# Three projections of a fused two-block layer in staggered runs: the second 128 tokens four weight pieces behind the first

## The reference, cut to what matters

```python
merged = sigmoid(ga) * (ya @ w_branch_a) + sigmoid(gb) * (yb @ w_branch_b)
mix_out = merged @ w_out
ple = sigmoid(x @ w_ple_gate) * (p @ w_ple)
x = layer_norm(DEEPNORM_ALPHA * x + mix_out + ple, ln_g, ln_b)      # end of block 1
...
h = rms_norm_2(x, g_mix_norm) * (1.0 + scale_m) + shift_m           # block 2
proj = h @ w_in                 # columns 0..415 and 1952..1959 are the narrow block "c0"
```

## Time and profile before

| | us |
|---|---|
| median of 3 runs | 1148.98 (1148.11 to 1151.58) |
| profiled execution, its own time | 1146.6 |
| its span | 1144.9 |
| PE busy | 1062.0 (93% of the span) |
| DVE busy | 550.1 (48%) |
| ACT busy | 390.1 (34%) |
| POOL busy | 335.6 (29%) |
| DMA | 320.65 MB, 280 GB/s over the span |

### The profile page before, as it was taken

The page is one execution under the profiler, slowest core; times in us unless marked ns, Lnnn a source line. Parts: engine busy times, 40 slices in busy tenths (PEclk is TensorE's granted clock), DMA queues, the critical chain, the costliest instruction groups (busy, mean ns, idle before and its releaser), DMA issues. The chain is left out here.

```text
span 1144.9 us, 12825 instructions
## 1 busy us (share of the span) xinstructions
PE 1062.0 (93%) x4990; PEld 705.6 (62%) x4990; DVE 550.1 (48%) x987; ACT 390.1 (34%) x668; POOL 335.6 (29%) x261
## 2 busy tenths in 40 slices
PE   6999999989999696999987999999999999999993
PEld 4887888768877565887776635353544444444442
DVE  5978677758765766655644312222222122222214
ACT  4645675546433424657333211121111111111212
POOL 1058946594683057274400000000000000000000
PEclk9999999989998797999996999999999999999997
DMA  9656653956675264455349389999999999999991
GB/s 327 207 184 221 221 202 111 338 178 252 199 275 186 74 194 147 128 172 204 112 185 376 120 343 416 412 417 418 417 418 417 417 416 417 416 417 417 418 374 38
DMA packets 93933, 320.65 MB, mean 280 GB/s; under 512 B 6288, under 2 KB 7328, under 8 KB 76976
## 3 DMA queue, kind: packets, MB, share of 16 engines
q1 hardware_dynamic: 92832, 316.07, 72.3%
q0 software_dynamic: 752, 3.22, 0.8%
q10 hardware_dynamic: 288, 0.52, 0.1%
HBM read 318.74 MB, written 1.05 MB: 279 GB/s over the span
## 5 line engine op out<-in xcount | busy, mean ns | idle before, releaser
L757 PE MATMUL ps<-hl,L 128*128 128x512 f32 (+1 forms) x1216 | 389.0, 402 | 11.8 <-DVE rlo L1501 8.5
L757 PEld LDWEIGHTS ps<-hl,L 128*128 128x128 f32 x1216 | 232.5, 194 | 60.9 <-issue 14.6
L1501 DVE TENSOR_TENSOR rlo<-ring,hl 128x1024 fp32r<-128x1024 f32 (+1 forms) x154 | 209.0, 1376 | 119.5 <-ACT hl L1164 118.7
L757 PE MATMUL ps<-rlo,L 128*128 128x512 f32 (+1 forms) x608 | 241.1, 397 | 0.0
L757 PE MATMUL ps<-slots_all,xe 128*64 128x512 f32 (+1 forms) x1056 | 226.9, 582 | 0.8 <-DVE rt L2236 0.8
L1164 ACT ACTIVATE hl<-ring 128x1024 fp32r<-128x1024 f32 (+1 forms) x154 | 159.9, 1057 | 196.6 <-PE ps L757 79.3
L718 POOL TENSOR_SCALAR ring<-ring,st 128x512 f32<-128x512 f32 x84 | 168.8, 2009 | 0.0
L746 POOL CAST two<-ident 64x128 fp32r<-64x128 f32 x64 | 19.1, 298 | 501.1 <-PE ps L757 499.6
L757 PEld LDWEIGHTS ps<-slots_all,xe 128*64 128x64 f32 x1056 | 73.9, 137 | 131.7 <-issue 128.5
L757 PEld LDWEIGHTS ps<-rlo,L 128*128 128x128 f32 x608 | 117.3, 193 | 25.0
L720 POOL TENSOR_TENSOR macc<-macc,ring 128x512 f32<-128x512 f32 x84 | 119.4, 1421 | 7.0
(11 more groups left out here) (208 smaller groups left out, 902.2 us busy)
## 6 DMA issues: line engine op xcount, KB each, us to landing
slots_all<-in_w_exp_gate SPq DMA_DIRECT2D x64, 1024.0 KB, 20.0
slots_all<-in_w_exp_up SPq DMA_DIRECT2D x64, 1024.0 KB, 15.9
slots_all<-in_w_exp_down SPq DMA_DIRECT2D x64, 1024.0 KB, 16.7
ring<-in_w_in SPq DMA_DIRECT2D x49, 1024.0 KB, 5.4
ring<-in_w_mod SPq DMA_DIRECT2D x24, 1024.0 KB, 7.3
ring<-in_w_out SPq DMA_DIRECT2D x8, 1024.0 KB, 5.1
ring<-in_w_ple_gate SPq DMA_DIRECT2D x4, 1024.0 KB, 5.2
ring<-in_w_branch_a SPq DMA_DIRECT2D x4, 1024.0 KB, 6.1
```

Of the source, the lines that this page charges most:

```text
L757: return e.matmul(o, l, r, start=start, stop=stop)
L1501: return e.tensor_tensor(o, a, b, op)
```

## The change

Names form runs: bb0 with bb1, wo0 with wo1, and c0 alone (`BEHIND`, lag 4). A run is a list of steps. In step s PE does piece s for m=0 and then piece s-4 for m=1. So a run of eight pieces has twelve steps: four with m=0 alone, four with both, four with m=1 alone; `c0` has eight steps. `pe_at`, `begun` and `used` give for every half its count and step; what frees a buffer is counted by `used`, the step in which m=1 has passed. The transposes, sums and norms are split by m and put between steps (`at`). The mean is a sum that DVE's addition accumulates, the variance a sum of squares by ACT with the mean as bias, and the last scaling isn't a DVE pass: `DIAG(m)`, the identity times 1/rms, is the moving operand of an ordinary float32 matmul that turns and scales R.

```diff
+        BEHIND = (("bb0 bb1", 4), ("wo0 wo1", 4), ("c0", 4),)
...
+                for s in range(len(ps) + lag):
+                    t = sum(len(v) for v in steps_of.values())
+                    halves = [(ps[s], 0)] if s < len(ps) else []
+                    halves += [(ps[s - lag], 1)] if s >= lag else []
+                    for g, m in halves:
+                        pe_at[(g, m)] = len(pe_at) + 1
+                        (used if m else begun)[g] = t
...
             if kind == "weights":
-                return last_piece[i] + 1
+                return used[last_piece[i]] + 1
...
-        for g in range(npieces):
+        for t, halves in (step for v in steps_of.values() for step in v):
             first = at_piece
-            while at_piece < min(g + NH, npieces) and all(
-                    freed_by(q) <= g for q in range(pieces[at_piece][0] - NS + 1)):
+            while at_piece < npieces and (at_piece < NH or used[at_piece - NH] < t) and all(
+                    freed_by(q) <= t for q in range(pieces[at_piece][0] - NS + 1)):
                 at_piece += 1
...
+            def spread_tokens(name, m, src, diag, ready):
+                for j0 in (0, 4):
+                    b = take((name, m, j0))
+                    ready(m, j0)
+                    for j in range(4):
+                        x = mm(b[:, 128 * j:128 * j + 128], src(m, j0 + j), diag(m), True, True)
+                    taken(x)
...
+            project("bb0", L0, l_ready("ybT"), {9: lambda: merged_turn(0)})
+            project("wo0", L1, l_ready("mT"), {1: lambda: merged_turn(1)})
+            h_turn(0)
+            project("c0", L0, h_ready, {2: lambda: h_turn(1)})
+            project("fq", L0, h_ready)
...
+            project("bb0", at={10: lambda: rounded("mT", tokens=(0,))})
+            def ln_square(m):
+                w.wait_ge(ln_v, 2 * m + 1)
+                act(UA[:, m, :], R[:, m, :], ACT.Square, bias=st[:, 74 + m:75 + m],
+                    accum_out=st[:, 168 + m:169 + m]).then_inc(ln_a, 1)
+                w.wait_ge(ln_v, 2 * m + 2)
                 act(st[:, 76 + m:77 + m], st[:, 76 + m:77 + m], ACT.Sqrt).then_inc(ln_a, 1)
...
+            project("wo0", at={2: first_rows, 7: lambda: ln_square(0), 8: first_squares, 9: roots})
+            h_round(0, 0)
+            square(1, 0)
+            h_round(0, 4)
+            square(1, 1)
+            square_root(1)
+            h_round(1, 0)
+            h_round(1, 4)
...
+            project("bb0", at={3: lambda: bb(0, 0), 7: after_bb1, 10: lambda: completed("mT", tokens=(0,))})
+            bb(1, 1)
...
+            def less_mean(m):
+                w.wait_ge(*evacuated("wo1", m))
+                mine(tt(st[:, 72 + m:73 + m], st[:, 160 + 2 * m:161 + 2 * m], st[:, 161 + 2 * m:162 + 2 * m], ALU.add))
...
+            def diagonal(m):
+                w.wait_ge(rt_a, m + 1)
+                mine(e.reciprocal(st[:, 70 + m:71 + m], st[:, 68 + m:69 + m]))
+                wait_mine()
+                tsc(DIAG(m), ident[:, :], st[:, 70 + m:71 + m], None, ALU.mult, None).then_inc(xn_set, 1)
...
+            def first_rows():
+                wo(1, 0)
+                less_mean(0)
+                variance(0)
+                wo(0, 1)
+                scale(0)
+                scaled(0, 0)
+                scaled(0, 1)
+
+            def second_rows():
+                w.wait_ge(sq_a, 2)
+                mean_square(0, rt_v)
+                wo(1, 1)
+                diagonal(0)
+                less_mean(1)
+                variance(1)
+                h_shift(0)
+                scale(1)
+                scaled(1, 0)
+                h_low(0, 0)
+                h_shift(4)
+                scaled(1, 1)
+                h_low(0, 4)
+
+            project("wo0", at={2: lambda: completed("mT", tokens=(1,)), 3: lambda: wo(0, 0), 7: first_rows, 9: second_rows})
+            w.wait_ge(sq_a, 4)
+            mean_square(1, rt_v)
+            diagonal(1)
+            h_low(1, 0)
+            h_low(1, 4)
```

More of the change, by code:

```diff
@@ L358, in two_blocks @@
         ev_a, ev_v = Events(sem("ev_a")), Events(sem("ev_v"))
-        for name in order:
-            for m in range(2):
+        for lead in steps_of:
+            for name, m in ((name, m) for m in range(2) for name in names_of[lead]):
                 dve = name.rstrip("01") in BY_DVE or (name in SHARED and m == 0)
@@ L413, in aux_turn, with aux_tokens, turn_order @@
                 aux((name, m, j0), by[n % len(by)])
+        def aux_tokens(name, m, by):
+            for j0 in (0, 4):
+                aux((name, m, j0), by)
+        BY_TOKENS = ("mT", "hT",)
+        def turn_order(name, groups):
+            if name in BY_TOKENS:
+                return [(j0, m) for m in range(2) for j0 in groups]
+            return [(j0, m) for j0 in groups for m in range(2)]
         HEADS_IN = {name: (s,) for s, name in enumerate("za1 ua0 ua1 va0 va1 zb0 zb1 gb0 gb1 ga0".split())}
@@ L499, in two_blocks @@
                              ("ofT", (0,)), ("mT2", (0, 4)), ("h3", (0, 4))):
-            for j0 in groups:
-                for m in range(2):
-                    th.add((name, m, j0))
+            for j0, m in turn_order(name, groups):
+                th.add((name, m, j0))
         for i in range(NP):
@@ L812, in between, with project @@
                     pair(4, FOX_IN[name][n], QM, KMT, 66, FV)
-            def project(name, L, ready):
-                for c in MOD_SUM.get(name, ()):
-                    mod_sum(c)
-                ps = blocks[name]
-                for n, g in enumerate(ps):
-                    w.wait_ge(hi, g + 1)
-                    w.wait_ge(lo, g + 1)
-                    hi_g, lo_g = hi_of(g), pieces[g][3]
-                    for m in range(2):
+            def project(lead, L, ready, at={}):
+                for name in names_of[lead]:
+                    for c in MOD_SUM.get(name, ()):
+                        mod_sum(c)
+                four = len(blocks[lead]) == 4
+                for s, (_, halves) in enumerate(steps_of[lead]):
+                    for g, m in halves:
+                        w.wait_ge(hi, g + 1)
+                        w.wait_ge(lo, g + 1)
+                        hi_g, lo_g = hi_of(g), pieces[g][3]
+                        name, n = block_of[g]
                         o = PS[bank_of[name] + m][:, 0:pieces[g][2]]
@@ L830, in project @@
                             mm(o, L[:, 1, kk, tok(m)], hi_g[:, k, :], False, False)
-                            x = mm(o, L[:, 0, kk, tok(m)], lo_g[:, k, :], False, kk == 2 * len(ps) - 1)
+                            x = mm(o, L[:, 0, kk, tok(m)], lo_g[:, k, :], False, kk == 2 * len(blocks[name]) - 1)
                         x.then_inc(pe_w, 1)
-                    if n == 1 and len(ps) == 4:
-                        between(name, 0)
-                between(name, 1 if len(ps) == 4 else 0)
+                    if s == 1 and four:
+                        between(lead, 0)
+                    if s in at:
+                        at[s]()
+                between(lead, 1 if four else 0)
             def scores(names, q, k, n):
@@ L1799, in head_norm, with completed @@
                     yield
-            def completed(name, groups=(0, 4)):
+            def completed(name, groups=(0, 4), tokens=(0, 1)):
                 for j0 in groups:
-                    for m in range(2):
+                    for m in tokens:
                         w.wait_ge(th.sem, th.at[(name, m, j0)])
@@ L1900, in _ @@
             project("ba1", branch("ba1", 1, GA, "ga1", None, None))
-            for c in range(2):
-                project(f"bb{c}", branch(f"bb{c}", c, GB, f"gb{c}", GA, merged))
-            completed("mT")
-            def wo(c):
-                def evac(m, b):
-                    o = R[:, m, half(c)]
-                    done(f"wo{c}", m)
-                    wait_mine()
-                    tt(o, b, o, ALU.add).then_inc(ev_v.sem, 1)
-                    w.wait_ge(*evacuated(f"wo{c}", m))
-                    mine(e.bn_stats(st[:, 160 + 12 * m + 6 * c:166 + 12 * m + 6 * c], o))
-                return evac
@@ L1915, in _, with bb, after_bb1 @@
-            for c in range(2):
-                project(f"wo{c}", wo(c))
+            def bb(m, *cs_):
+                for c in cs_:
+                    branch(f"bb{c}", c, GB, f"gb{c}", GA, merged)(m, PS[bank_of[f"bb{c}"] + m][:, :])
+            def after_bb1():
+                bb(0, 1)
+                bb(1, 0)
+            project("bb0", at={3: lambda: bb(0, 0), 7: after_bb1, 10: lambda: completed("mT", tokens=(0,))})
+            bb(1, 1)
+            mine(stt(Am, modcol[:, 1, :], 1.0, cols[:, 48:56], ALU.add, ALU.mult))
@@ L1928, in _, with scale, scaled @@
+            def scale(m):
+                w.wait_ge(ln_a, 2 * m + 2)
                 mine(e.reciprocal(st[:, 78 + m:79 + m], st[:, 76 + m:77 + m]))
                 wait_mine()
-                for c in range(2):
-                    o = R[:, m, half(c)]
```

(4 more changed lines are left out.)

195 lines of the change are left out of this document (115 added, 80 removed).

## The result

The changed kernel takes **1141.0 us** (median of 7 runs, 1137.06 to 1144.44), the kernel before 1148.98 in the same comparison: ratio 0.9937, 95% interval 0.9915 to 0.9959. That is 8.0 us less (4.7 to 9.8 by the interval); forecast were 5.0 less, 1144, in 1137 to 1153.

A forecast was written before the change was run, and what follows sets the result against it. PE was taken as the bound, busy 1062.0 of 1144.9 us, with holes that also cost the clock. Terms -4.0 - 0.9 - 4.8 + 2.1 + 2.5 = -5.1 from 1146.6 gave 1141.5; with 2.4 for the median, 1144, range 1137 to 1153.

The forecast's parts named there:

- A: Branch b up to the start of wo: wo starts at 345.3 in place of 349.27, -4.0 us.
- B: The wo run: 22.9 us with the clock up, in place of 23.85, -0.9 us.
- C: From wo's end to c0's end: 23.3 us in place of 28.1, -4.8 us.
- D: Behind c0: fk's first load waits for a later buffer, so conversion and reading of c0 come later, +2.1 us.
- E: Behind fq, before the up-projections: the longer hole makes the clock fall, cold for some 5 us, +2.5 us.
- the holes close: Rival, wo to fq: faster conversions, early diagonal, clock holds in c0 and behind fq; -11.9 us, 1137; chance 0.20.
- starved: Rival, wo's start and c0: buffers freed too late, 1.5 us delay, clock falls; +4.2 us, 1153; chance 0.16.
- Given back behind c0: Rival: late reading of c0 costs 3.5, low clock 3.5, c0 at half clock to its end; -0.4, 1148.5; chance 0.17.
- The diagonal isn't cheaper: Rival, c0's chain: float32 products cost 0.37 and more, 16 add 2 us; 1146, inside the forecast's range, no own chance.

The follow-up runs named there:

- e3: Changed kernel with the turned first half of the merged branches rounded and completed at step 8, not 10, of the branch run: 1141.2 us.
- e4: Changed kernel with c0 not staggered, both turns ahead of it, the two other staggers kept: 1146.43 us.
- e9: Changed kernel with the first half's mean square, root and diagonal ahead of one conversion and the other half's addition: 1141.56 us.
- e1: Changed kernel with fk's first piece converted in fq's first step, behind the reading of c0: 1137.12 us.
- e2: Changed kernel with four extra float32 products, their result overwritten, filling PE's hole before the up-projections: 1140.35 us.
- e8: Changed kernel with only the diagonal undone: DVE scales all 1024 columns and PE transposes; stagger and sums kept: 1140.29 us.
- e7: Changed kernel with all three staggers undone, sums by accumulation and the diagonal kept: 1150.81 us, ratio to before 1.0021.
- e10: Changed kernel with e1's and e9's edits, plus first rows modulated and completed earlier and the second diagonal ahead of two conversions: 1135.81 us.
- e11: e10 with e3's edit added: 1133.34 us, ratio to before 0.9873.

## Why the prediction was right, point by point

Sizes from the trace of after, on before's scale:

| part | forecast | measured |
|---|---|---|
| A, start of wo | 345.3, -4.0 | 345.9, -3.4 |
| B, wo run | 22.9, -0.9 | 24.6, +0.75 |
| C, wo end to `c0` end | 23.3, -4.8 | 22.7, -5.4 |
| D, `c0` end to up-projections | +2.1 | +2.1 (16.0 against 13.9) |
| E, clock behind fq | +2.5 | +1.5 |
| sum | -5.1 | -4.5 |

**A** is right in size and in its cause: the hole before wo is 2.23 us (forecast 2.4), DVE's rounding ends it. (Its lower bound, 343.8, is a slip: 335.5 with four conversions of 1.23, the two sums and 0.68 gives 344.6, so -4.7, and *the holes close* would be 1138.) The modulation sum took 2.08 us at full clock, not the 1.04 that was assumed; DVE hid that in A.

**B** is the step that failed: "22.9 with the clock up". The clock fell to 0.50 between 347.5 and 348, after 2.08 us of one-column matmuls and 2.23 us idle, and the run took 1.7 us longer than forecast. The term behind it is that modulation sum, halved by the forecast as if its time followed the clock: it counted 3.4 us without dense work, less than the 3.9 us after which the clock had fallen at 377.0, and took the clock to hold. It was 4.3 us. That is the description of the rival *starved*, without its extra delay of 1.5 us. e3, in which the clock stays up there, is no faster (1141.2), since `c0`'s load and DVE's list come next.

**C** came out 0.6 better in length, by errors that cancel, and that is luck. The first diagonal matmul came 1.7 us after the forecast's 371.3 (372.98), because wo ended late; the diagonal hole was 2.52 (forecast 3.1). The clock was down for 10.9 us after the restart at 374.32, not 7 to 8.6, and came back near 383.9 on before's scale, not 380. `c0`'s end, 393.1, is 1.6 after the forecast's 391.5. The diagonal matmul was sized well: eight in 1.95 us at full clock, 0.24 each (0.25), and 3.78 at half clock in e4, 0.47 (0.45); the 3.22 in after began at full clock. What sets the start of `c0` is DVE's list to its first operand as a whole, not the chain to the first diagonal: in e9 that diagonal's turn comes 1.9 us earlier than in after, and `c0` starts where it did (72.55 against 72.51 from `ybT`).

**D** is exact and its cause shown twice: e1 takes it away (hole 1.46), and e4, in which `c0` isn't staggered, has the old hole back (2.05).

**E**: the clock fell as forecast, and the price on the products was well sized: 11.53 us in place of 8.83, 2.7 more (forecast 2.5). But the forecast passed all of it on, and the hole before the next transposes took up 1.2 of it, so that 1.5 us were left there (434.11 - 410.47 = 23.6 against 437.29 - 415.19 = 22.1 in before):

```profile
437.29 2.55 PE L761 MATMUL ps<-ident,bs 128*96 128x128 f32 x16 [2.34 <-DVE bs L1501]
```

In e2, which takes the low clock away, 1.3 us come back at these transposes and 0.7 in the median. Why the clock falls is less sure than the forecast had it: in e4 it fell with the old hole.

In the prediction the rule of the Trainium skill, "TensorE: Matmul & The Clock Gate", section "Part 4: PE-mode transpose", that a transpose doesn't count as work for the clock as a matmul does, was taken to mean that the new turn, an ordinary matmul, would bring the clock back an us or so earlier in `c0`. The runs don't show it. In after the clock is up again in the window 384 to 386; a mean of 0.70 puts the rise near 385.2, 78.2 counted from `ybT`. In e8, with transposes in that turn, this is the window:

```profile
382.00:384.00 2.00, 2.00 (x10) 0.68 0.07 29
```

Here 0.68 puts the rise near 383.3, 78.6 counted from e8's `ybT` (304.65), and `c0` itself began 0.3 later there (72.84 against 72.51). So the ordinary matmuls brought the clock back at most half a us earlier, and the time shows no difference. For the transposes behind fq the runs decide nothing: with the same six as PE's last work the clock fell in after and e4 and held in before, e1 and e7. Further on, a trace speaks against the rule. The reader sees PE in after idle for 7.24 us, then with nothing but sixteen transposes, and the clock back at 1.00 before they end:

```profile
443.27 3.58 PE L806 MATMUL ps<-ident,bs 128*96 128x128 f32 x16 [7.24 <-DVE bs L1908]
```

```profile
446.50:447.00 0.50, 0.50 (x6) 0.86 0.00 0
```

The mean of 0.86 puts the rise near 446.6; the next matmul starts at 446.69. The measurement decides: here the clock came back over transposes alone.

**The total** fell by 8.0, not by 5.0. The interval reaches to 4.7, so the forecast isn't contradicted. But its premise that all later stages shift by one amount holds only from 645 us on: the last 499.9 us are equal in before and after. Ahead of that the traces differ, counted from `ybT`:

| kernel | next transposes | group behind a hole, 518.11 in after | transposes, 574.87 in after | end of the span |
|---|---|---|---|---|
| before | 131.66 | 218.24 | 271.95 | 839.27 |
| after | 127.14 | 211.14 | 267.90 | 835.73 |
| e4 | 131.92 | 219.17 | 272.86 | 840.05 |
| e7 | 137.94 | 224.37 | 277.99 | 844.97 |
| e1 | 123.12 | 207.51 | 261.29 | 829.10 |
| e10 | 120.10 | 204.19 | 261.03 | 828.79 |
| e11 | 120.15 | 204.28 | 258.10 | 825.94 |

To the first column the gain is the 4.5 us of the parts above. To the second it is 7.1: the stage between takes 84.0 us in after and 86.6 in before, because the clock, which is at 0.50 when PE restarts behind a hole of some 7 us, comes back 3.4 us after the restart in after and 9 in before:

```profile
446.47 3.65 PE L761 MATMUL ps<-ident,bs 128*96 128x128 f32 x16 [6.63 <-DVE bs L1813]
```

```profile
454.00:456.00 2.00, 2.00 (x7) 0.63 0.00 0
```

All nine kernels with `c0` staggered have the short stage (83.9 to 84.5), the three without the long one (86.4 to 87.3). So some 2.6 us of the gain belong to a place that the forecast has no term for. Why the clock comes back sooner there isn't shown, and that the change brings it is luck. To the third column after loses 3.0 us again: its clock fell at two later holes (0.72 in 517 to 520, 0.55 in 559 to 562), where before kept 1.00 over holes as long:

```profile
518.11 1.90 PE L802 MATMUL ps<-macc,ones 128*128 128x512 f32 x2 [1.43 <-ACT ex L1232]
```

```profile
523.87 1.12 PE L757 MATMUL ps<-macc,ones 128*128 128x512 f32 x2 [1.51 <-ACT ex L1164]
```

e10 and e11 reach that place within 0.1 us of each other; in e10 the clock fell and in e11 it held, and that is the 2.9 us between them. How many of the other executions of before and after had such a fall no trace shows, so how the 8.0 us divide between the change and this remains open.

Of the signs named for the forecast, the hole before wo, that before the first diagonal, fk's conversion 3.3 us behind `c0`'s end and the hole of 4 us at low clock came; wo's start was 0.9 us late (345.9), `c0`'s end 1 to 2 us (393.1), and the later stages did not shift by one amount. Of the rivals, *the holes close* is refuted (three holes remain, the clock fell at all). *Given back behind c0* is too large: the delay was 2.1 us, not 3.5, and `c0` didn't run at half clock to its end. *Starved* is right about the clock at wo's start and wrong about the delay that it needs. *The diagonal isn't cheaper* is right for the half clock only (0.47 each; 0.24 at full), and costs nothing (e8).

## What to carry to other kernels

A stagger of token halves pays by giving a long chain of small vector operations another half's matmuls to hide behind; the cheaper operations inside the chain were worth nothing here without it, and the one of them that was undone alone, the diagonal, made no difference with it. When a hole closes, look at the whole ordered list of the engine that ended it, not at the last wait: the hole before the first diagonal could be removed for no gain, while reordering the same operations gave 2 us. And a buffer that the stagger frees later moves the load behind it, whose conversion then blocks whatever stands behind it in an in-order list; one condition that moved that conversion gave 3.9 us between the medians.

A stage can also gain or lose some 3 us by the clock alone, far from the change. Count stages from a common mark, and look at where two traces part, before a difference of totals is put down to the edit.

## What the runs showed of the hardware that was not expected

- Sixteen one-column float32 matmuls took 2.08 us at clock 1.00 (342.88 in after) and 2.08 at 0.50 (377.47 in after, 388.16 in the earlier trace rows): their time didn't follow the clock.
- In e10 PE stood only 1.45 us, behind such a group of 2.08 us, and the clock fell:

```profile
372.00:374.00 2.00, 1.45 (x13) 1.00 0.34 131
374.00:376.00 2.00, 1.10 (x4) 0.76 0.00 0
376.00:378.00 2.00, 2.00 (x7) 0.50 0.00 0
```

  In e1, 1.46 us idle behind fq and six transposes left it at 1.00. Behind those same transposes it held over 2.18 us (before) and 2.08 (e7) and fell with 2.05 (e4). So a hole's length alone doesn't tell whether the clock falls. Whether the group ahead matters in e10 wasn't tried.
- The clock came back to 1.00 in after near 446.6, when PE had done nothing but float32 transposes since its restart at 443.27.
- The clock isn't a function of the program alone: the seven runs of after have a mean granted clock between 0.961 (1144.44 us) and 0.968 (1137.06 us), and spread over 7.4 us, nearly as much as this change is worth.
- DVE reads an accumulator in 0.08 us (356.04 in after), ACT in 0.19; DVE scaled 1024 columns from SBUF by a column in 0.75 us (e8), where 0.92 was assumed.
